# First RMSNorm of a hybrid decoder step: the raw rows turned by TensorE first, and the norm weight and row factor multiplied in afterwards

## The chip, the cores and the metric

The kernel runs on one core of one Trainium2 chip, in fp32. The metric is the device time of one execution in microseconds; three runs of the kernel before gave 590.5, 587.02 and 591.28 us. PE is TensorE, DVE is VectorE, ACT is ScalarE, POOL is GpSimd, SP is SyncE, which here mostly issues transfers.

## What is computed

One inference step of a two-layer decoder trunk over 320 tokens: a prompt of 256 and a sample group of 8 x 8. Layer 0 is sliding-window attention beside an S5 state space model, layer 1 is an RG-LRU beside dilated attention, and each is followed by a mixture of experts (16 experts, 2 per token). Every part begins with an RMSNorm of the residual rows. The change is in the first of them.

```python
def rmsnorm(x, g):
    xf = x.astype(F32)
    y = xf * lax.rsqrt(jnp.mean(xf * xf, axis=-1, keepdims=True) + RMS_EPS)
    return (y * g.astype(F32)).astype(x.dtype)

def even_mixer(h, kv_cache, s5_state, p, table):     # h = rmsnorm(x, norm_mix[0])
    proj = h @ p['w_in']                             # q, k, v for attention, u for S5
    ...
    ob, h_last = s5_mixer(u, h0, p)                  # lam_bar, b_bar and their powers: tables
```

## The kernel before, in words

The program is four blocks in a row: even_mixer_block (layer 0), moe_block, odd_mixer_block, moe_block. Within a block each engine has its own instruction stream, written out by hand, and waits on semaphores. An engine's stream is in order, so whatever stands behind a waiting instruction waits too.

The 320 tokens lie as rows in `resid`, in three tiles t = 0, 1, 2 of 128, 128 and 64 rows (`ROWS`), each row 1024 long. The projections need the normalised rows turned, with the 1024 features on the partitions: `xnT`, 8 chunks of 128 features by 320 tokens. The opening stage makes it so:

- SP issues, in this order, a small table input (L458), the three row tiles (L461), the norm weights and other columns (`small`, L462), the weights `w_u` (L152, from L463), the S5 B and C matrices (L464) and `w_qkv` (L152, from L465).
- POOL builds the identity matrix `ident` (L509 to L512).
- ACT and DVE make each row's sum of squares: DVE for tile 0 (L918), ACT for tiles 1 and 2 (`square`, L787). ACT takes the root of the mean (`root`, L793).
- DVE's `scale(t)` (L884 to L888) takes the reciprocal of the root and writes `rdiag[t]`, a diagonal matrix: the identity times the row factors.
- PE waits for tile 0 and for `ident`, runs three filler matmuls of 256 columns (`keep_clock_up`, L182; their results are not used), and then turns and scales in one step: for each tile eight matmuls of a 128-feature chunk of raw rows against `rdiag[t]` (L587), four to each of two PSUM banks, x0a, x0b, x1a, x1b, x2a, x2b.
- DVE's `gain(t)` (L890 to L899) multiplies each bank by the norm weight in one tensor_tensor of up to 512 columns (L896) and writes `xnT`. The weight is broadcast along the tokens, so one instruction serves four chunks.
- When x2b is emptied and `w_u` is there, PE starts the projections u0 to u3 (L577), then q0, eight banks of transposes of the S5 table `wt` (L602), q1, q2, the `tau` matmuls (L614), which need the S5 table `cp` that DVE finishes at L989, and then V (L625), q3, k and v.

An fp32 matmul is two MATMUL records in the profile and a transpose is one; so L587 has 24 matmuls and 48 records.

Between these steps DVE computes the small columns of the S5 discretisation (den, n1, cr, ci; L925 to L944; 16 columns each), and from L949 on it builds the large tables: `bbar`, `bbd`, `wt` (L970 to L975) and `cp` (L983 to L989). In the kernel before, den to cr (L925 to L935) stand between `scale(0)` and `scale(1)`, and three more (L942 to L944) behind the last gain. `Link` makes DVE wait for its own last instruction.

Names and lines that the steps touch: `rdiag` (L315), the semaphores (L402 to L405), POOL's identity (L509 to L512), PE's opening (L580 to L590), DVE's `scale` and `gain` (L884 to L899) and DVE's order of work (L924 to L944).

## Time and profile before

| | |
|---|---|
| three runs | 590.5, 587.02, 591.28 us; median 590.5 |
| span of the profiled execution | 585.1 us |
| PE busy | 560.8 us, 96% of the span |
| PEld (weight load) busy | 312.1 us, 53% |
| DVE busy | 250.1 us, 43% |
| ACT busy | 154.6 us, 26% |
| POOL busy | 77.0 us, 13% |
| moved by DMA | 208.96 MB, a mean of 357 GB/s |

The profiled execution's span runs from its first to its last instruction; the three runs are timed from outside and are 2 to 6 us longer. Start times in the rows below are us from the span's start. A row of the view in order of time gives the start, the time to the end of the last instruction of the group, engine, line, operation, output and input, shape and count; behind them, in brackets, the idle time before it and what ended it.

### The profile page before, as it was taken

Reading aid. Unit: us, or ns where it says so; the run is one execution under the profiler, and the core shown is the slowest. Engines: PE = TensorE matmul, PEld = TensorE weight load, DVE = VectorE, ACT = ScalarE, POOL = GpSimd, SP = SyncE. Lnnn points to the kernel's source line nnn. Section 1 sums busy time; section 2 is a strip of 40 time slices with the busy share of each in tenths; the row PEclk is TensorE's granted clock in tenths of the full one; section 3 lists DMA queues with packets and bytes.
Section 4 is the critical chain, followed back from the end, with each engine's and each line's share of the span. In section 5 each row is a group of like instructions: output and inputs, shape, how many; then the busy total and the mean of one; then the engine's idle time right before and its main releaser. Section 6 shows DMA issues by size and latency. Waiting matters only on the chain. (4 is left out here: it accounts for less than half of the span.)

```text
span 585.1 us, 8567 instructions
## 1 busy us (share of the span) xinstructions
PE 560.8 (96%) x3450; PEld 312.1 (53%) x3450; DVE 250.1 (43%) x595; ACT 154.6 (26%) x327; POOL 77.0 (13%) x116
## 2 busy tenths in 40 slices
PE   6999999999999999999999999999999899999992
PEld 5777876543633333337876556567644633333330
DVE  6999783224642112145633415350113751211147
ACT  6132195121301111134235105063013301011022
POOL 5940800000212110000000001000000021210000
PEclk9999999999999999999999999999999999999998
DMA  8995999997999999999999998999699989999982
GB/s 328 415 351 79 233 392 374 374 414 297 366 393 418 419 421 418 392 284 401 395 408 330 414 380 328 311 369 404 235 424 418 398 343 407 422 417 422 370 230 90
DMA packets 40074, 208.96 MB, mean 357 GB/s; under 512 B 12835, under 2 KB 14563, under 8 KB 24192
## 3 DMA queue, kind: packets, MB, share of 16 engines
q1 hardware_dynamic: 30560, 169.93, 75.1%
q0 software_dynamic: 7872, 34.53, 16.4%
q10 hardware_dynamic: 1600, 3.90, 1.7%
q8 instruction: 30, 0.49, 0.3%
q14 instruction: 12, 0.10, 0.0%
HBM read 198.77 MB, written 43.74 MB: 414 GB/s over the span
## 5 line engine op out<-in xcount | busy, mean ns | idle before, releaser
L1510 PE MATMUL bank<-arena 128*64 128x512 f32 x264 | 85.4, 598 | 0.2 <-DVE arena L1850 0.2
L1510 PE MATMUL bank<-ring,arena 128*64 128x512 f32 x232 | 74.4, 598 | 0.2 <-DVE arena L1850 0.2
L2326 PE MATMUL bank<-arena,ring 128*128 128x320 f32 x256 | 71.6, 434 | 0.0
L2326 PEld LDWEIGHTS bank<-arena,ring 128*128 128x128 f32 x256 | 48.0, 190 | 21.3 <-issue 1.6
L1431 PE MATMUL bank<-ring,arena 128*128 128x512 f32 x92 | 40.3, 594 | 1.0 <-PEq L455 0.6
L1510 PEld LDWEIGHTS bank<-arena 128*64 128x64 f32 x264 | 24.2, 136 | 31.4 <-issue 31.3
L1541 PE MATMUL bank<-arena 128*64 128x512 f32 x136 | 39.8, 594 | 0.7 <-ACT arena L1764 0.7
L577 PE MATMUL bank<-xnT,ring 128*128 128x320 f32 x144 | 39.5, 434 | 0.5 <-DVE xnT L896 0.5
L1984 DVE COPY arena<-bank 128x512 f32<-128x512 f32 x14 | 9.7, 692 | 68.3 <-PE bank L1541 68.3
L1541 PE MATMUL bank<-ring,arena 128*64 128x512 f32 x120 | 36.1, 593 | 0.7 <-ACT arena L1764 0.7
L1510 PEld LDWEIGHTS bank<-ring,arena 128*64 128x64 f32 x232 | 21.2, 136 | 24.7 <-issue 24.5
L577 PEld LDWEIGHTS bank<-xnT,ring 128*128 128x128 f32 x144 | 27.1, 190 | 11.6 <-DVE xnT L896 0.7
L1762 ACT ACTIVATE arena<-bank 128x256 f32<-128x256 f32 x16 | 6.1, 384 | 91.0 <-PE bank L1510 91.0
L1431 PEld LDWEIGHTS bank<-ring,arena 128*128 128x128 f32 x92 | 17.2, 190 | 22.7 <-issue 22.7
L1978 DVE TENSOR_TENSOR arena<-arena,bank 128x256 f32<-128x256 f32 x16 | 6.7, 421 | 51.9 <-ACT arena L1762 51.9
L1859 DVE TENSOR_TENSOR arena<-bank,small 128x512 f32<-128x512 f32 x28 | 18.1, 687 | 20.3 <-PE bank L1492 20.1
L1767 ACT COPY arena<-bank 128x512 f32<-128x512 f32 x16 | 9.4, 586 | 65.0 <-PE bank L1541 65.0
L1400 POOL DMA_INDIRECT y_rows<-arena x12 | 12.1, 1004 | 110.1 <-DVE arena L1984 110.1
L1541 PEld LDWEIGHTS bank<-arena 128*64 128x64 f32 x136 | 12.3, 136 | 20.7 <-issue 20.3
L2382 PE MATMUL bank<-ring,arena 128*128 128x512 f32 (+1 forms) x64 | 21.2, 489 | 0.0
L1746 ACT ACTIVATE arena<-resid 128x1024 f32<-128x1024 f32 (+1 forms) x6 | 6.3, 1058 | 54.8 <-DVE resid L1825 54.8
L1541 PEld LDWEIGHTS bank<-ring,arena 128*64 128x64 f32 x120 | 11.3, 136 | 16.3 <-issue 15.9
(450 smaller groups left out, 853.1 us busy)
## 6 DMA issues: line engine op xcount, KB each, us to landing
arena<-in_w_moe SPq DMA_DIRECT2D x50, 1024.0 KB, 16.8
ring<-in_w_moe SPq DMA_DIRECT2D x44, 1024.0 KB, 15.4
arena<-in_stream_b SPq DMA_DIRECT2D x4, 2560.0 KB, 14.6
out_o_d_old<-in_cache_d_g POOLq DMA_DIRECT2D x1, 8448.0 KB, 29.8
arena<-in_stream_a SPq DMA_DIRECT2D x4, 2048.0 KB, 10.4
out_o_d_old<-in_cache_d_g POOLq DMA_DIRECT2D x1, 7680.0 KB, 44.4
out_o_d_old<-in_cache_d_g SPq DMA_DIRECT2D x1, 4608.0 KB, 37.5
ring<-in_w_out_even SPq DMA_DIRECT2D x2, 2048.0 KB, 11.2
```

The lines of the kernel that those rows point to most:

```text
L577: last = nc.tensor.matmul(bank(name)[:, 0:TOK], lhs(k), c.xnT[:, k, :], start=(k == 0), stop=(k == KC - 1))
L1400: pool.indirect_dma_start(out=x["y_rows"], out_offset=bass.IndirectOffsetOnAxis(ap=scatter_idx[:, j:j + 1], axis=0), in_=yo_of(j), in_offs ...
L1431: last = nc.tensor.matmul(c.bank[2 * t + h][:, :], parts[q][:, t * P:(t + 1) * P], where[q][:, h * 512:(h + 1) * 512], start=(q == 0), sto ...
L1510: last = nc.tensor.matmul(c.bank[2 + j % 2][half, :], xgT[:, j % 2, q, half], w[i][q // 4][:, q % 4, :], start=(q == 0), stop=(q == KC - 1))
L1541: last = nc.tensor.matmul(c.bank[4 + h][half, :], hidT[:, j % 2, f, half], w[i][:, f, h * 512:(h + 1) * 512], start=(f == 0), stop=(f == 1))
L1746: nc.scalar.activation(xn[0:rows, t], c.resid[0:rows, t], ACT.Square, accum_out=c.stat[0:rows, t:t + 1]).then_inc(sq_ok, 1)
L1767: nc.scalar.copy(yo_of(j)[:, 0:512], c.bank[4][:, :]).then_inc(yo_a, 1)
L1859: v.tensor_tensor(xgT[:, j % 2, 4 * h:4 * h + 4, :], c.bank[h][:, :].rearrange("p (k r) -> p k r", k=4), c.gains[:, gain, 4 * h:4 * h + 4] ...
L1978: v.tensor_tensor(hid[:, j % 2], sg[:, j % 2], c.bank[2 + j % 2][:, FF:2 * FF], ALU.mult).then_inc(hid_ok, 1)
L1984: v.tensor_copy(yo_of(j)[:, 512:D], c.bank[5][:, :]).then_inc(yo_b, 1)
L2326: last = nc.tensor.matmul(bank(name)[:, 0:TOK], w[:, k, i * P:(i + 1) * P], xnT[:, k, :], start=(k == 0), stop=(k == KC - 1))
L2382: last = nc.tensor.matmul(bank(f"v{2 * t + n}")[:, 0:m], xnT[:, k, t * P:(t + 1) * P], wv[:, k, c0:c0 + m], start=(k == 0), stop=(k == KC ...
```

## The change

PE no longer waits for the row factors before it turns the rows. It turns each raw tile with plain transposes against `ident` as soon as that tile has landed (`turn_raw`). The row factors reach the other side by a second way: `row_factor(t)` is one matmul whose stationary operand is the column of factors broadcast to 128 columns and whose moving operand is `ident`; it leaves in bank 7, on every partition, the row of 128 (or 64) factors. DVE copies that row to SBUF (`factor`) and then multiplies each 128-feature chunk by the norm weight (a scalar per partition) and by the row of factors in one scalar_tensor_tensor: eight small instructions a tile in place of two large ones. `rdiag` is gone, `scale(t)` is the reciprocal alone. The three filler matmuls ahead of the turning go, and two stand behind each `row_factor` instead. On DVE the steps are interleaved, and most of the small S5 columns (the reciprocal of den to cr, and one more) move behind the last gain. POOL's wait inside the identity is written with another semaphore and is otherwise the same.

```diff
--- before.py
+++ after.py
@@ -312,7 +312,7 @@
     t["oS"] = f[:, 2560:2816]
     g = ar.take(4096)
     t["xn"] = g[:, 0:3 * D].rearrange("p (t d) -> p t d", t=3)
-    t["rdiag"] = g[:, 3 * D:3 * D + 3 * P].rearrange("p (t k) -> p t k", t=3)
+    t["factor"] = g[:, 3 * D:3 * D + TOK]
     t["win"] = g.rearrange("p (j r m) -> p j r m", r=2, m=P)
     t["S1"] = g[:, 0:2048].rearrange("p (h k) -> p h k", h=A_H)
     t["PT1"] = g[:, 2048:4096].rearrange("p (h b k) -> p h b k", h=A_H, b=2)
@@ -399,10 +399,11 @@
     ld_bc, ph_ok = c.sem("e_b_and_c"), c.sem("e_first_phases")
     ld_kc, ld_late, ld_bias = c.sem("e_kc"), c.sem("e_late"), c.sem("e_bias")
     full, a_empty, d_empty = c.sem("e_bank_full"), c.sem("e_act_emptied"), c.sem("e_dve_emptied")
-    ident0, ident_ok, bbd0, wuu0 = c.sem("e_ident0"), c.sem("e_ident"), c.sem("e_bbd0"), c.sem("e_wuu0")
+    ident_ok, bbd0, wuu0 = c.sem("e_ident"), c.sem("e_bbd0"), c.sem("e_wuu0")
     p_own, d_own, a_own = c.sem("e_pool_own"), c.sem("e_dve_own"), c.sem("e_act_own")
     dt_ok, arg_ok, trig_ok = c.sem("e_dt"), c.sem("e_arg"), c.sem("e_trig")
     sq_ok, rms_ok, xn_ok = c.sem("e_sq"), c.sem("e_rms"), c.sem("e_xn")
+    factor_pe = c.sem("e_pe_row_factor")
     lam_ok, pw_ok, rho_ok = c.sem("e_lambda"), c.sem("e_powers"), c.sem("e_rho")
     bbd_ok, wt_ok, cp_ok, h_ok = c.sem("e_bbd"), c.sem("e_wt"), c.sem("e_cp"), c.sem("e_h")
     u_out, u_in, wuu_in = c.sem("e_u_out"), c.sem("e_u_in"), c.sem("e_wuu_in")
@@ -418,7 +419,7 @@
     cp, wuu, wt, win, U, H, tau, y40 = (ev[n] for n in ("cp", "wuu", "wt", "win", "U", "H", "tau", "y40"))
     kcT, vc, bias, S0, SS, S1 = (ev[n] for n in ("kcT", "vc", "bias", "S0", "SS", "S1"))
     PT0, PTs, PTn, PT1, pw, ph, rho = (ev[n] for n in ("PT0", "PTs", "PTn", "PT1", "pw", "ph", "rho"))
-    rdiag = ev["rdiag"]
+    factor = ev["factor"]
     yT, ygT, xn, bbar, bbd, oS, vs = (ev[n] for n in ("yT", "ygT", "xn", "bbar", "bbd", "oS", "vs"))
     logdt, a_re, a_im = (ev["in"][:, PAIRS * q:PAIRS * (q + 1)] for q in range(3))
     braw, ct = (ev["in"][:, 3 * PAIRS + 512 * q:3 * PAIRS + 512 * (q + 1)].rearrange("p (r j c) -> p r j c", r=2, c=GC)
@@ -506,8 +507,7 @@
         @block.gpsimd
         def _(pool):
             g, link = nc.gpsimd, Link(pool, p_own)
-            g.memset(c.ident[:, :], 0.0).then_inc(ident0, 1)
-            pool.wait_ge(ident0, 1)
+            link(g.memset(c.ident[:, :], 0.0))
             g.affine_select(out=c.ident[:, :], in_=c.ident[:, :], compare_op=ALU.not_equal, fill=1.0,
                             base=0, pattern=[[-1, P]], channel_multiplier=1).then_inc(ident_ok, 1)
             g.memset(c.stat[:, 0:16], 1.0)
@@ -577,17 +577,32 @@
                     last = nc.tensor.matmul(bank(name)[:, 0:TOK], lhs(k), c.xnT[:, k, :], start=(k == 0), stop=(k == KC - 1))
                 last.then_inc(full, 1)
 
-            pe.wait_ge(ident_ok, 1)
-            pe.wait_ge(ld_x[0], 16)
-            c.keep_clock_up(c.bank[7], 3, 256)
-            for t, rows in enumerate(ROWS):
-                pe.wait_ge(xn_ok, t + 1)
+            def turn_raw(t):
+
+                rows = ROWS[t]
+                pe.wait_ge(ld_x[t], 16)
                 for h in range(2):
                     for k in range(4):
-                        last = nc.tensor.matmul(bank(f"x{t}{'ab'[h]}")[:, k * rows:(k + 1) * rows],
-                                                c.resid[0:rows, t, (4 * h + k) * P:(4 * h + k + 1) * P], rdiag[0:rows, t, 0:rows],
-                                                start=True, stop=True)
+                        last = nc.tensor.transpose(bank(f"x{t}{'ab'[h]}")[:, k * rows:(k + 1) * rows],
+                                                   c.resid[0:rows, t, (4 * h + k) * P:(4 * h + k + 1) * P], c.ident[0:rows, 0:rows])
                     last.then_inc(full, 1)
+
+            def row_factor(t):
+
+                rows = ROWS[t]
+                pe.wait_ge(xn_ok, t + 1)
+                nc.tensor.matmul(c.bank[7][:, t * P:t * P + rows], c.stat[0:rows, 6 + t:7 + t].broadcast_to([rows, P]),
+                                 c.ident[0:rows, 0:rows], start=True, stop=True).then_inc(factor_pe, 1)
+
+            pe.wait_ge(ident_ok, 1)
+            for t in range(3):
+                turn_raw(t)
+            row_factor(0)
+            c.keep_clock_up(c.bank[6], 2, 256)
+            row_factor(1)
+            c.keep_clock_up(c.bank[6], 2, 256)
+            row_factor(2)
+            c.keep_clock_up(c.bank[6], 2, 256)
             emptied(pe, "x2b")
             c.arrived(pe, IT_U)
             for i in range(4):
@@ -884,19 +899,20 @@
             def scale(t):
 
                 dve.wait_ge(rms_ok, t + 1)
-                link(v.reciprocal(c.stat[:, 6 + t:7 + t], c.stat[:, 3 + t:4 + t]))
-                v.tensor_scalar(rdiag[:, t], c.ident[:, :], c.stat[:, 6 + t:7 + t], None, ALU.mult).then_inc(xn_ok, 1)
-
-            def gain(t):
-
-                rows = ROWS[t]
-                for h in range(2):
-                    name = f"x{t}{'ab'[h]}"
-                    filled(dve, name)
-                    v.tensor_tensor(c.xnT[:, 4 * h:4 * h + 4, t * P:t * P + rows],
-                                    bank(name)[:, 0:4 * rows].rearrange("p (k r) -> p k r", k=4),
-                                    c.gains[:, 0, 4 * h:4 * h + 4].unsqueeze(2).broadcast_to([P, 4, rows]), ALU.mult)\
-                        .then_inc(d_empty, 1)
+                v.reciprocal(c.stat[:, 6 + t:7 + t], c.stat[:, 3 + t:4 + t]).then_inc(xn_ok, 1)
+
+            def gain(t, h):
+
+                rows, name = ROWS[t], f"x{t}{'ab'[h]}"
+                if h == 0:
+                    dve.wait_ge(factor_pe, t + 1)
+                    link(v.tensor_copy(factor[:, t * P:t * P + rows], c.bank[7][:, t * P:t * P + rows]))
+                filled(dve, name)
+                for k in range(4):
+                    last = v.scalar_tensor_tensor(c.xnT[:, 4 * h + k, t * P:t * P + rows], bank(name)[:, k * rows:(k + 1) * rows],
+                                                  c.gains[:, 0, 4 * h + k:4 * h + k + 1], factor[:, t * P:t * P + rows],
+                                                  ALU.mult, ALU.mult)
+                last.then_inc(d_empty, 1)
 
             dve.wait_ge(dt_ok, 1)
             v.tensor_tensor(x1, a_re, dt, ALU.mult).then_inc(arg_ok, 1)
@@ -921,24 +937,26 @@
             v.tensor_tensor(li, ex, sn, ALU.mult)
             v.tensor_tensor(lr, ex, cs, ALU.mult).then_inc(lam_ok, 1)
             dve.wait_ge(lam_ok, 1)
-            scale(0)
             v.tensor_tensor(t1s, a_re, a_re, ALU.mult)
             link(v.tensor_tensor(t2s, a_im, a_im, ALU.mult))
+            scale(0)
             link(v.tensor_tensor(den, t1s, t2s, ALU.add))
+            link(v.tensor_scalar(n1, lr, -1.0, None, ALU.add))
+            dve.wait_ge(ld_small, 16)
+            gain(0, 0)
+            scale(1)
+            gain(0, 1)
+            gain(1, 0)
+            scale(2)
+            gain(1, 1)
+            gain(2, 0)
+            gain(2, 1)
             link(v.reciprocal(den, den))
-
-            link(v.tensor_scalar(n1, lr, -1.0, None, ALU.add))
             v.tensor_tensor(t1s, n1, a_re, ALU.mult)
             link(v.tensor_tensor(t2s, li, a_im, ALU.mult))
             link(v.tensor_tensor(t1s, t1s, t2s, ALU.add))
             v.tensor_tensor(cr, t1s, den, ALU.mult)
             link(v.tensor_tensor(t2s, li, a_re, ALU.mult))
-            scale(1)
-            dve.wait_ge(ld_small, 16)
-            gain(0)
-            scale(2)
-            gain(1)
-            gain(2)
             link(v.tensor_tensor(t1s, n1, a_im, ALU.mult))
             link(v.tensor_tensor(t2s, t2s, t1s, ALU.subtract))
             link(v.tensor_tensor(ci, t2s, den, ALU.mult))
```

## Rows read from the trace of the kernel before

**Rows 1.** The page: span and busy time by engine
```profile
span 585.1 us, 8567 instructions
PE 560.8 (96%) x3450; PEld 312.1 (53%) x3450; DVE 250.1 (43%) x595; ACT 154.6 (26%) x327; POOL 77.0 (13%) x116
```
**Rows 2.** Busy by stretch: PE, PEld, DVE, ACT, POOL, granted clock, DMA share, GB/s
```profile
14.75:112.00 97.25, 97.17 (x904) 73.26 (x905) 73.11 (x116) 37.75 (x97) 33.70 (x32) 1.00 0.95 320
112.00:545.00 433.00, 424.83 (x2375) 220.66 (x2376) 148.75 (x419) 98.46 (x193) 33.55 (x42) 1.00 0.96 380
```
**Rows 3.** Waits of PE up to 120 us: us in total, times, longest
```profile
PE bank L577 <- DVE xnT L896: 0.5, 1, 0.5
```
**Rows 4.** In order of time, the opening stage
```profile
4.81 2.90 PE L182 MATMUL bank<-resid,ident 128*128 128x256 f32 x6 [4.81 <-DMA resid<-in_x_prompt]
7.02 0.16 DVE L887 RECIPROCAL stat<-stat 128x1 f32<-128x1 f32 x1 [0.75 <-ACT stat L793]
7.61 0.79 PE L587 MATMUL bank<-arena,resid 128*128 128x128 f32 x2
...
9.83 1.41 DVE L896 TENSOR_TENSOR xnT<-bank,small 128x512 f32<-128x512 f32 x2
14.27 0.42 DVE L896 TENSOR_TENSOR xnT<-bank,small 128x256 f32<-128x256 f32 x1 [0.47 <-PE bank L587]
14.75 21.80 PE L577 MATMUL bank<-xnT,ring 128*128 128x320 f32 x80 [0.52 <-DVE xnT L896]
15.27 0.42 DVE L949 TENSOR_TENSOR ring<-arena 128x256 f32<-128x256 f32 x1
```
**Rows 5.** In order of time, SP's issues of the row tiles and of w_u
```profile
1.20 0.89 SPq L461 DMA_DIRECT2D resid<-in_x_prompt  x2
2.13 0.57 SPq L461 DMA_DIRECT2D resid<-in_x_sample  x1
3.36 0.43 SPq L152 DMA_DIRECT2D ring<-in_w_u  x1
```
**Rows 6.** DMA issues of the same: count, KB each, median us from issue to landing
```profile
resid<-in_x_prompt SPq DMA_DIRECT2D x2, 512.0 KB, 4.1
resid<-in_x_sample SPq DMA_DIRECT2D x1, 256.0 KB, 5.4
ring<-in_w_u SPq DMA_DIRECT2D x1, 2048.0 KB, 9.1
```
**Rows 7.** In order of time, later on: the same filler, and transposes
```profile
152.48 1.03 PE L182 MATMUL bank<-resid,ident 128*128 128x256 f32 x4
36.39 3.66 PE L602 MATMUL bank<-ident,arena 128*128 128x128 f32 x32
148.08 0.70 PE L1450 MATMUL bank<-ident,resid 64*128 64x64 f32 x8 [0.42 <-DVE resid L1825]
```
**Rows 8.** Busy by stretch, columns as in Rows 2, while PE turns the tiles
```profile
10.00:11.00 1.00, 1.00 (x11) 1.00 (x10) 0.95 (x2) 0.93 (x3) 0.84 (x4) 1.00 0.92 393
```
**Rows 9.** In order of time: DVE, small steps with a scalar column, copies from PSUM
```profile
286.05 0.48 DVE L2683 SCALAR_TENSOR_TENSOR arena<-arena,small 128x256 f32<-128x256 f32 x1
286.45 0.28 DVE L2684 SCALAR_TENSOR_TENSOR arena<-arena,small 128x64 f32<-128x64 f32 x1
...
97.75 0.29 DVE L1079 COPY arena<-bank 128x128 f32<-128x128 f32 x1 [2.62 <-PE bank L749]
...
102.97 0.49 DVE L1082 COPY arena<-bank 128x128 f32<-128x128 f32 x2 [3.71 <-PE bank L764]
```
**Rows 10.** In order of time: the end of cp, the start of tau, DVE's next slack
```profile
45.05 2.56 DVE L989 SCALAR_TENSOR_TENSOR arena<-arena,ring 128x2304 f32<-128x2304 f32 x1
48.59 1.63 PE L614 MATMUL bank<-arena 128*32 128x128 f32 x52
69.89 1.29 DVE L1035 SCALAR_TENSOR_TENSOR arena<-bank,ring 128x512 f32<-128x512 f32 x2 [3.12 <-PE bank L645]
```
**Rows 11.** Instructions on bank, 4 to 20 us: ns min/median/max, first and last start
```profile
L587 PEld LDWEIGHTS bank<-arena,resid x48: 183/192/333, 7.6 to 13.9; 128*128 128x128 f32 x32, 64*128 64x128 f32 x16
```

## Prediction

> **What bounds the kernel now.** I read the page first: PE is busy for 560.8 of 585.1 us, and no other engine for half of that [rows 1]. Busy time alone doesn't say that PE sets the end, so I read the stretches next: from 14.75 to 112 us PE works for 97.17 of 97.25 us, and up to 545 us for 424.83 of 433 [rows 2]. From the first projection on PE has hardly a gap, so when that projection starts is worth its whole shift, unless something behind it comes late. PE's waits up to 120 us name, besides the first row tile, 0.5 us for DVE's last gain [rows 3]; the tile is there at 4.81 [rows 4]. The change lies in between, so the question is: when does the first projection (L577) start, 14.75 us before?
>
> The opening in order of time [rows 4] shows four things. Tile 0 is there at 4.8 us. The first row factor is there at 7.02 + 0.16 = 7.2, and PE turns with it from 7.61. DVE starts its gains at 9.83 and ends them at 14.27 + 0.42 = 14.69, 4.9 us later, with idle time in between because it waits for PE: PE sets the pace, DVE follows. w_u, issued at 3.36 [rows 5], takes 9.1 us [rows 6] and lands at 12.5; that is the earliest start a faster opening could reach, a gain of 2.2 us at most.
>
> **PE's clock.** The granted clock stands at 1.00 in every stretch [rows 2], but the fillers tell more. Six records of 256 columns take 2.90 us from 4.81 on [rows 4], and four of the same take 1.03 us at 152.48 [rows 7]. Taking away about 0.6 and 0.4 us for the last one's own length, one follows the other after 0.45 and 0.21 us: the slow level (1.2 GHz) at the start, the fast one (2.4 GHz) later. The rise lies between: from 10 to 11 us already 11 records of 128 columns run, less than 0.1 us each [rows 8], against 0.23 at the fillers' pace. PE had worked since 4.8 us. The projections are fast: 80 records of 320 columns in 21.80 us are 0.27 us each [rows 4].
>
> **The change, part by part, by its place in time.**
>
> *Turning the raw rows.* Removed are three fillers and the wait for the factor; added are 24 transposes. Tile 0 is there at 4.8; tile 1 is issued about 0.45 us after 1.20 and takes some 4.6 us (4.1 is the median of the two, and tile 0 took 3.6), so 6.3; tile 2 lands at 2.13 + 5.4 = 7.5 [rows 5, 6]. Fast, 32 transposes of 128 columns take 3.66 us, 0.11 each, and eight of 64 rows take 0.70, that is 0.07 each and 0.2 for the last one's length [rows 7]. PE is on the slow level here, and I take twice that: 16 x 0.227 = 3.6, then 8 x 0.13 = 1.1, and 4.8 + 4.7 = 9.5 us. The lower bound is the fast price: tile 2 is then the last to land, and 7.5 + 0.6 = 8.1.
>
> *The row factor stands behind all of them.* row_factor(0) is in PE's stream behind the 24 transposes, tile 2's wait included. Its input is ready at 7.3 and it runs at 9.5. A single fp32 matmul of 128 columns on the slow level is two records, 0.79 us from start to end [rows 4]. So DVE gets its first factor at 10.3 (lower bound 8.1 + 0.5 = 8.6), against 9.83 for its first bank before. The early turning buys nothing, since the factor doesn't come earlier than the matmul it replaces. DVE meanwhile has only den and n1 left, and idles from 8 to 10.3.
>
> *DVE's multiplications.* Removed are 6 large tensor_tensor (1.41 us for two of 512 columns [rows 4], so 4 x 0.7 + 2 x 0.42 = 3.6 us) and three rdiag of 0.3. Added are 24 scalar_tensor_tensor, 16 of 128 columns and 8 of 64, and three copies. The nearest rows, with the same kind of scalar column, are L2683 and L2684: 256 columns let the next start after 0.40 us [rows 9]. If a column costs 1/960 us, as from 256 to 64 columns (0.48 - 0.28 = 0.20 us for 192), then 0.133 us of it are fixed. A step of 128 costs 0.27 and one of 64 costs 0.20: 16 x 0.27 + 8 x 0.20 = 5.9 us. Copies: 0.29, 0.29 and 0.22 with 0.05 each for the link, 0.95. Reciprocals of tiles 1 and 2: 0.16 each, 0.32. Sum 7.2 us. The lower bound goes by copies of 128 columns without a scalar column, of which the second starts 0.20 after the first (two of 0.29 in 0.49 [rows 9]): 16 x 0.20 + 8 x 0.13 + 1.3 = 5.5. The upper bound, no overlap at all, is 0.35 and 0.28 a step: 9.1 us.
>
> *Are the later factors in time?* Tile 1's reciprocal stands behind gain(0, 0), so at 10.3 + 0.3 + 1.1 + 0.2 = 11.9. PE's two fillers run from 9.9 to 11.7, so it is free; the factor is out at 12.75, and DVE wants it at 12.95. For tile 2 the same sum gives 15.35 against 15.6. Both are hidden by gain(t, 1), with 0.2 us to spare; every tenth more on PE beyond that costs a tenth, twice.
>
> *The first projection.* 10.3 + 7.2 = 17.5, and 0.05 for the semaphore: 17.55 against 14.75, **2.8 us later**. w_u has long landed.
>
> *The moved S5 columns.* Nine small steps now stand behind the last gain where three stood. I take 0.21 each, estimated from the row factor's reciprocal of 0.16 [rows 4] and 0.05 for the link, 1.85 us in all. Table building starts at 17.5 + 1.85 = 19.3 instead of 15.27 [rows 4], 4.0 us later. From there DVE is busy without pause until cp ends at 45.05 + 2.56 = 47.6; PE wants it at 48.59 [rows 10]. PE is 2.8 late and has 1.0 to spare, 3.8 together, so the tau matmuls wait **0.2 us** more. Behind them DVE has 3.12 us of idle time at the first scores [rows 10], which takes up its remaining 1.0. The removed fillers cost PE nothing, since it waited then; the new ones lie in its waits for DVE. POOL's edit changes only a semaphore's name.
>
> **Sum.** 2.8 + 0.2 = 3.0 us, made against the profiled 585.1: 588.1. The median of the runs is 5.4 us above that execution, so 590.5 + 3.0 = **593.5 us**, 0.5% more. A measurement of this kernel can tell about 1% from no change, that is 5.9 us; the three runs alone lie 4.3 us apart.
>
> **Rivals.**
>
> *The clock has fallen, or never risen, when the projections start* (chance 0.13). Before, PE ran real matmuls without a pause from 4.8 us. After, 24 transposes come first, and then fillers with pauses; if the clock rises only for the latter, the projections may start slow. Before, PE was fast by 10 us [rows 8], some 5 us after its first matmul; if as much of the projections runs at half speed, 2.5 us are lost, so 3.0 + 2.5 = 5.5, and 596.0. Against it: from 9.5 us on the factor matmuls and fillers keep PE at work with short pauses only, for longer than it had worked before when it became fast. A rule speaks for this rival. The Trainium skill, page "TensorE: Matmul & The Clock Gate", Part 4, says that transposes don't count as work for the clock gate. The kernel before shows no stretch of transposes at the slow level, so its trace doesn't decide it; by the rule the clock's rise would only begin to be earned at 9.5.
>
> *Not slower: the opening is cheap* (chance 0.17). If transposes cost their fast price though the clock is slow, and DVE's steps come 0.20 apart, DVE starts at 8.6 and needs 5.5: 14.1, so 0.6 us earlier than before, and 589.9. It decides from the point where the first factor's time and DVE's steps add up to 14.7. With only one of the two true it is 590.5 + 1.1 or 1.3, and 591.7. Against it: while PE turned, the longest weight load took 333 ns and the median one 192 [rows 11], so I read the 333 as the slow level's, and the nearest steps with a scalar column have the larger fixed part. On this too a rule speaks otherwise: the Trainium skill, the same page, Part 2, gives a weight load of 128 columns about 107 ns, whatever the clock. By it tile 2's transposes would end at 8.4, the first factor would reach DVE at 9.2, and the sum would be 1.9 us instead of 3.0.
>
> *The shift is taken up later* (0.07): a wait on a transfer behind 14.75 us would make the change nothing, 590.5. Against it: PE's waits name none up to 120 us [rows 3].
>
> *DVE's tables become the bound* (0.03): if the moved columns or the slower gains make DVE more than 5 us late, tau waits for the difference, 1 to 2 us: 595. It starts at a lateness of DVE that is 1.0 us larger than PE's.
>
> **How the numbers follow.** The forecast keeps 0.60. Its own range is 592 to 595; with the cheap opening and the slow clock it is 589.9 to 596, and as medians of three runs move by some 2 us, I give 588.5 to 596.5. Faster by over 1% (under 584.6) is out of reach of every case, since w_u allows 2.2 us: 0.02. Slower by over 1% (over 596.4) needs the slow clock and high runs, or DVE's steps at their upper bound with it: 0.07. The rest, 0.91, is within 1%.
>
> **What would show it.** In the trace after: the last raw transpose starts near 9.4 and the first factor matmul follows; the first copy of the factor row is near 10.3, behind about 2 us of DVE idle time; steps of 128 columns start 0.27 apart; the first projection starts near 17.5 with 80 records in 21.8 us (more would be the slow clock); cp ends near 51.6, and tau starts just behind it. The forecast is wrong if the first factor comes by 8.6, if the steps are 0.20 apart, if the projections run at 0.45 us a record, or if the MoE stages begin at the old time although the projections don't.

## The result: 0.6% slower, and where it went

Over 13 runs each, the kernel before has a median of 589.93 us and the changed kernel of 592.45 us. Compared run for run the changed kernel takes 1.0062 times as long, 95% interval 1.0041 to 1.0082, which is 2.4 to 4.8 us. The forecast was 3.0 us more (1.0051) and 593.5 us. Ratios here and below leave out a run that lies more than 1.5% above the fastest of the same kernel: one of 660.39 us of the kernel before, and one of 594.03 us of the last version below.

The opening of the changed kernel, in order of time (start, length, engine, line, operation, shape, count; in brackets the idle time before and its end):

```profile
4.56 4.52 PE L586 MATMUL bank<-ident,resid 128*128 128x128 f32 x24 [4.56 <-DMA resid<-in_x_prompt]
...
7.07 0.16 DVE L902 RECIPROCAL stat<-stat 128x1 f32<-128x1 f32 x1 [0.45 <-ACT stat L808]
...
9.01 0.49 PE L594 MATMUL bank<-ident,stat 128*128 128x128 f32 x2
...
9.34 1.03 PE L182 MATMUL bank<-resid,ident 128*128 128x256 f32 x4
...
9.63 0.29 DVE L909 COPY arena<-bank 128x128 f32<-128x128 f32 x1 [2.05 <-PE bank L594]
...
9.96 1.13 DVE L912 SCALAR_TENSOR_TENSOR xnT<-bank,small,arena 128x128 f32<-128x128 f32 x4
...
14.80 1.62 DVE L912 SCALAR_TENSOR_TENSOR xnT<-bank,small,arena 128x64 f32<-128x64 f32 x8
...
16.48 5.92 PE L577 MATMUL bank<-xnT,ring 128*128 128x320 f32 x21 [1.32 <-DVE xnT L912]
...
18.22 0.42 DVE L967 TENSOR_TENSOR ring<-arena 128x256 f32<-128x256 f32 x1
```

These answer to [rows 4]. The factor is ready at 7.23 and its matmul runs at 9.01, behind all 24 transposes; DVE stands idle for 2.05 us until it can copy the factor row. From there to the end of its last small step at 16.42 it has no gap. The first projection starts at 16.48 instead of 14.75, 1.7 us later. The tables start at 18.22 instead of 15.27, 2.95 later.

The second stretch to look at lies between 18 and 57 us, where I had forecast almost nothing. In the kernel before its main steps are these:

```profile
17.81 0.85 DVE L962 COPY arena<-arena 64x512 f32<-64x512 f32 x2
...
32.84 3.51 POOL L549 MEMSET arena<- 128x4096 f32 x1
...
48.59 1.95 PE L614 MATMUL bank<-arena 128*32 128x128 f32 x64
```

In the changed kernel, again in order of time:

```profile
19.89 3.51 POOL L549 MEMSET arena<- 128x4096 f32 x1
20.32 0.42 DVE L972 TENSOR_TENSOR arena<-ring 128x256 f32<-128x256 f32 x1
20.78 3.34 DVE L980 COPY arena<-arena 64x512 f32<-64x512 f32 x2
...
41.61 8.78 PE L577 MATMUL bank<-xnT,ring 128*128 128x320 f32 x32
...
50.45 2.56 DVE L1007 SCALAR_TENSOR_TENSOR arena<-arena,ring 128x2304 f32<-128x2304 f32 x1
...
53.11 3.34 PE L629 MATMUL bank<-arena 128*32 128x128 f32 x64 [2.72 <-issue]
56.38 3.93 PE L640 MATMUL bank<-ring,arena 128*64 128x40 f32 x128
```

Two copies of 64x512 (they build `bbd`) take 3.34 us; in the kernel before two of them take 0.85. They begin while POOL's memset of 4096 columns is on (19.89 to 23.40) and end after it. In the kernel before that memset comes 13 us later, long behind the copies. So cp is ready at 50.45 + 2.56 = 53.01 instead of 47.61 [rows 10], 5.4 us later. PE is through with its projections at 50.39 and waits 2.72 us for it. Then the tau matmuls (L629) take 3.34 us, where those of the kernel before take 1.95: most of them at half speed. V (L640) starts at 56.38 instead of 50.47, so PE is now 5.9 us late: 1.7 from the opening, 2.7 from the wait, 1.4 from the slow tau, and 0.1 left over.

The stretches of PE show the clock's fall (length, busy time, granted clock, DMA share, GB/s):

```profile
50.40:53.10 2.70, 0.00 (x0) 0.91 0.00 0
53.10:56.40 3.30, 3.29 (x66) 0.56 0.02 5
56.40:60.20 3.80, 3.80 (x132) 1.00 0.03 6
```

The granted clock is 0.56 while the tau matmuls run, near the 1.2 GHz level, and 1.00 behind them. It fell within the 2.7 us in which PE stood idle (0.91 on the mean of that stretch).

The profiled pair is 6.8 us apart (585.1 and 591.9), more than the comparison of runs says. A second profile of each (below) gave 586.4 and 590.5, 4.1 us apart, as are their first MoE stages (114.42 and 118.54). The spread of single executions is part of what a single pair shows: over the profiles of all the kernels here, the stretch from the start of the first MoE stage to the end takes 471.3 to 474.6 us, and 478.5 in one.

### The profile page after: what moved, and what is told of

Read it like the earlier page. It is cut to its first block and busy times, and to the rows that moved or that the text cites. A ratio compares the mean times of both kernels' runs of the same rounds, so it can differ in the third digit from the quotient of the medians.

```text
span 591.9 us, 8563 instructions
## 1 busy us (share of the span) xinstructions
PE 561.6 (95%) x3438; PEld 311.8 (53%) x3438; DVE 254.6 (43%) x613; ACT 154.5 (26%) x327; POOL 64.0 (11%) x116
```

## The experiments

Each ratio is against the kernel before on the same chip. "Tables", "cp" and "tau" are the start of DVE's tables, the end of cp, and the start of the tau matmuls.

### POOL's memset later

```diff
+            pool.wait_ge(wt_ok, 2)
             g.memset(wuu, 0.0).then_inc(wuu0, 1)
```

> The changed kernel with one wait more: POOL clears wuu only when DVE has finished wt. Theory A (port collision): in the changed kernel POOL's 3.51 us memset from 19.89 holds up DVE's first bbd copy (2.90 us for what took about 0.43), cp ends 2.5 us later for it, tau waits 2.7 us and then runs slow (3.34 for 1.95 us). So here: first projection unchanged at 16.5, the two copies back to 0.85 us, cp ends near 50.6 instead of 53.0, tau waits 0.3 us at most and takes 1.95; the time falls by 3.5 to 4 us from the changed kernel's 592.5. Theory B (the moved columns alone make the tables late; the copy's length has another cause): cp and time don't move. Theory C (the profiled pair is 6.8 us apart by the spread of runs): no change in the median.

Measured: ratio 1.0026 (1.0002 to 1.0050), median 589.91. In order of time:

```profile
20.74 0.85 DVE L981 COPY arena<-arena 64x512 f32<-64x512 f32 x2
...
35.36 3.52 POOL L550 MEMSET arena<- 128x4096 f32 x1 [15.43 <-DVE arena L994]
...
47.93 2.56 DVE L1008 SCALAR_TENSOR_TENSOR arena<-arena,ring 128x2304 f32<-128x2304 f32 x1
...
50.59 1.95 PE L630 MATMUL bank<-arena 128*32 128x128 f32 x64
```

The opening is unchanged (first projection at 16.55), and everything behind it is as theory A wants: the copies back to 0.85 us, cp at 50.49, tau at 50.59 behind q2, at full speed. V starts at 52.47, 3.9 us earlier than in the changed kernel's first profile and 2.7 earlier than in its second (55.18, below), where tau ran at full speed. The time fell by 0.36% (1.0062 to 1.0026), some 2 us, less than the 3.5 to 4 that I expected: the slow tau, 1.4 of them, isn't in every run. The two intervals still overlap a little; that the collision is gone rests on the trace, and the size on the runs. The memset of 3.5 us lies here under DVE steps with two inputs (the cp tables), which keep their 2.55 us: it holds up only the copies.

### The copies as steps with two inputs

```diff
-                last = v.tensor_copy(bbd[...], bbar[rows])
+                last = v.tensor_tensor(bbd[...], bbar[rows], bbar[rows], ALU.max)
```

> The changed kernel with its two bbd copies (64x512) written as a tensor_tensor of bbar with itself (max), the same result, POOL's memset left where it is. In the changed kernel the tensor_tensor steps at 19.86 and 20.32 ran in their usual 0.42 us with the memset already on, and only the copy stood still. Theory A1 (the memset and a one-input DVE step exclude each other, a two-input step isn't held): both steps take about 0.6 us, cp ends near 50.7, tau waits 0.3 us at most, the time is that of the kernel with the late memset (589.9, 2 us less than the changed kernel). Theory A2 (any DVE step of that size is held while POOL clears): 2.9 us as before, cp at 53, no change.

Measured: ratio 1.0029 (1.0001 to 1.0058). The memset is where it was, and the two steps lie inside it:

```profile
19.30 3.51 POOL L549 MEMSET arena<- 128x4096 f32 x1
...
21.43 1.38 DVE L980 TENSOR_TENSOR arena<-arena 64x512 f32<-64x512 f32 x2
...
51.80 1.95 PE L629 MATMUL bank<-arena 128*32 128x128 f32 x64 [0.69 <-ACT arena L834]
```

1.38 us for two (0.69 each; two two-input steps of 512 columns take 1.41 in [rows 4]), nothing held, and cp at 51.70. That is 1 us later than expected: the first projection started at 17.21 here, since PE was at the slow level until past 12.5 us, and tau waited 0.69 us instead of 0.3 at most. Theory A1 holds: a one-input copy and the memset exclude each other, a two-input step and the memset don't. The ratio is that of the late memset; its interval is too wide to part it from the changed kernel by itself.

### The S5 columns back ahead of the gains

```diff
             link(v.tensor_scalar(n1, lr, -1.0, None, ALU.add))
+            link(v.reciprocal(den, den))
+            ... (t1s, t2s, cr, t2s)
             gain(0, 0)
             ...
             gain(2, 1)
-            link(v.reciprocal(den, den))
-            ... (t1s, t2s, cr, t2s)
```

> The changed kernel with the S5 columns (reciprocal of den to cr, and one more) back ahead of the gains, where DVE idles for 2 us. Theory A: first projection unchanged at 16.5, tables start at 17.0 instead of 18.2; the copies then start near 19.5, the second one still meets POOL's memset at 19.9, so cp ends between 51.7 and 52.5 and the time falls by about 0.7 to 1.5 us. Theory B: the whole lateness of the tables is the columns: cp ends 1.3 us earlier at 51.7, and the time falls by 1.3 us; nothing is left that a memset could explain.

Measured: ratio 1.0042 (1.0017 to 1.0067). In its profile:

```profile
16.78 8.63 PE L577 MATMUL bank<-xnT,ring 128*128 128x320 f32 x20 [1.33 <-DVE xnT L912]
...
19.94 0.95 DVE L980 COPY arena<-arena 64x512 f32<-64x512 f32 x2
...
20.55 3.79 POOL L549 MEMSET arena<- 128x4096 f32 x1
```

The tables started at 17.37 and the copies came just ahead of the memset, so the collision, which I had expected for the second one, didn't happen: this time POOL was held a little (3.79 for 3.51). cp ended at 49.78, 3.2 us earlier than in the changed kernel: 0.85 because the tables started earlier, 2.4 because the copies weren't held. Theory B, without a memset in it, had 51.7. But PE wasn't there to use it: 20 records of the projections took 8.63 us, 0.43 each, where the changed kernel's take 0.27. PE's clock fell in the pause of 1.33 us ahead of them (granted clock 0.94 from 15.4 to 16.1 us, 0.50 from 16.1 to 16.7), and the w transposes started at 41.40, 24.6 us behind the first projection instead of 21.6: the slow-clock rival, in one execution, at a price of 3.0 us. The runs show a gain of 0.2% over the changed kernel, less than the half-width of the interval, and can't decide between the theories; the trace speaks for A.

### Both repairs

The two edits together.

> The changed kernel with both repairs: S5 columns ahead of the gains, POOL's memset behind wt. What is left against the kernel before is the opening alone: first projection at 16.5 to 17.2 against 14.75, copies 0.85 us, cp near 49.4, no wait at tau. If the account is complete the time lies 1.7 us (0.3%) above the kernel before, as with the late memset alone (1.0026), since cp was then already just in time; if the columns had a cost of their own, it is lower than that by 0.3% and equals the kernel before.

Measured: ratio 1.0005 (0.9980 to 1.0030). First projection at 16.21, tables at 16.71, copies 0.86 us, cp at 49.00, tau at 50.05 without a wait, first MoE stage at 115.29 against 113.83 and 114.42 in the two profiles of the kernel before. What the opening itself costs is thus 0.9 to 1.5 us in the profile, and too little for the runs to tell. I expected 1.0026 if the columns cost nothing by themselves, and a ratio of 1 if they did. The interval holds both. By the profiles they cost little: the kernel with the late memset alone starts its MoE stage at 115.82, 0.5 us later, and 0.3 of that is there at its first projection.

### The column order alone, in the kernel before

```diff
             link(v.tensor_tensor(den, t1s, t2s, ALU.add))
-            link(v.reciprocal(den, den))
             link(v.tensor_scalar(n1, lr, -1.0, None, ALU.add))
-            ... (t1s, t2s, cr, t2s)
             scale(1)
             ...
             gain(2)
+            link(v.reciprocal(den, den))
+            ... (t1s, t2s, cr, t2s)
```

> The kernel before with only the order of DVE's S5 columns changed, as in the changed kernel. The first projection stays at 14.75 or comes 0.2 us earlier. Tables start near 16.5 instead of 15.3. Theory B: cp ends 1.2 us later, 48.8, tau waits 0.2 us, time up by 0.2 us. Theory A: POOL's memset, no longer held up by DVE's large steps, starts near 19.9, just as the bbd copies (19.1 to 19.9) end; if it catches the second one, cp ends near 51, tau waits 2.5 us and the time rises by 2.5 to 4 us; if it starts behind them, 0.2 us.

Measured: ratio 1.0006 (0.9981 to 1.0030). Tables at 16.42, copies at 19.02 to 19.88, free, cp at 48.81, tau at 48.91, 0.3 us later than in the kernel before: the 0.2 us of theory B, and 0.1 that this execution's first projection (14.85) was late. POOL's memset came at 22.61, because DVE's large steps, from 19.91 on, still reached the last small step of POOL's chain and held it for 2.24 us. The move of the columns is harmless alone; it takes the 1.7 us of the opening with it to open the gap in which POOL runs ahead.

### The first factor early

```diff
-            for t in range(3):
-                turn_raw(t)
-            row_factor(0)
+            turn_raw(0)
+            row_factor(0)
+            turn_raw(1)
+            turn_raw(2)
```

> The changed kernel with row_factor(0) right behind the transposes of tile 0 instead of behind all 24. My step said the first factor is late because it stands behind them: then the first factor row is copied near 8.2 instead of 9.6, and the first projection starts near 15.1 instead of 16.5. Tile 1's and 2's transposes are done by 10.4, in time for gain(1, 0). If DVE is held by something else (the later factors, or the steps), the start moves by under 0.5 us. On the time: 1.4 us less, or less than that where the tables (cp) set tau's start, since they also move by 1.4 us but may meet POOL's memset otherwise.

Measured: ratio 1.0041 (1.0020 to 1.0061).

```profile
4.55 1.94 PE L586 MATMUL bank<-ident,resid 128*128 128x128 f32 x8 [4.55 <-DMA resid<-in_x_prompt]
7.25 0.80 PE L594 MATMUL bank<-ident,stat 128*128 128x128 f32 x2 [0.76 <-DVE stat L903]
...
10.73 2.07 PE L182 MATMUL bank<-resid,ident 128*128 128x256 f32 x4
12.59 0.64 PE L594 MATMUL bank<-ident,stat 128*128 128x128 f32 x2
...
13.27 0.29 DVE L910 COPY arena<-bank 128x128 f32<-128x128 f32 x1 [2.54 <-PE bank L594]
...
17.66 7.61 PE L577 MATMUL bank<-xnT,ring 128*128 128x320 f32 x21 [1.32 <-DVE xnT L913]
```

Half of the expectation came true: the first factor row was copied at 8.18, 1.5 us earlier. The first projection didn't follow: it started at 17.66, not near 15.1. PE was still at the slow level at 10.7: the two fillers (four records) took 2.07 us instead of 1.03, row_factor(1) stood behind them, and DVE waited 2.54 us for its second factor. Whether the pause of 0.76 us ahead of the early factor kept the clock down isn't shown; two profiles without that pause were also slow at 9.4 us (below). The step is right that the factor is late for standing behind the transposes; in this execution undoing it only moved the wait to the next factor. The projections too ran in part at the slow level (granted clock 0.53 from 17.6 to 20 us), and yet the tau matmuls started at 53.18, as in the changed kernel (53.11): up to there cp sets the time, and a late PE is hidden. So this run doesn't price the order of the factors.

### Large steps in place of small ones

The norm weight is left out here, so a half tile needs one step, and the results are not those of the kernel; it serves as a price only:

```diff
-                for k in range(4):
-                    last = v.scalar_tensor_tensor(c.xnT[:, 4 * h + k, ...], bank(name)[...], c.gains[...], factor[...], ...)
+                last = v.tensor_tensor(c.xnT[:, 4 * h:4 * h + 4, ...], bank(name)[...], factor[...].unsqueeze(1).broadcast_to([P, 4, rows]), ALU.mult)
```

> The changed kernel with the late memset, and with the norm weight left out: each half tile is multiplied by the factor row alone, in one tensor_tensor of up to 512 columns instead of four scalar_tensor_tensor. It prices the step count by itself. If the 24 small steps are what the opening loses, DVE's gains take 4 x 0.62 + 2 x 0.35 = 3.2 us instead of 5.8, the first projection starts near 14.0 instead of 16.5, ahead of the 14.75 of the kernel before, and the time is 2.5 us under that of the kernel with the late memset (589.9) less what tau's wait for cp takes back. If the wait for the first factor is what is lost, the start moves by under 1 us.

Measured, with the late memset also in: ratio 0.9985 (0.9952 to 1.0018), against 1.0026 with the late memset alone: 2.4 us less, 2.5 expected, with intervals that overlap a little.

```profile
9.81 0.69 DVE L912 TENSOR_TENSOR xnT<-bank,arena 128x512 f32<-128x512 f32 x1
...
13.82 13.46 PE L578 MATMUL bank<-xnT,ring 128*128 128x320 f32 x49
```

The first projection started at 13.82, where the kernel with the late memset alone has 16.55. So the small steps cost 2.7 us of the opening, and the opening is 0.9 us ahead of the kernel before, in spite of the late first factor. A kernel that multiplies by the norm weight as well would need more than this; no run here prices it.

### No fillers

```diff
-            c.keep_clock_up(c.bank[6], 2, 256)      (three times)
```

> The changed kernel without its six filler matmuls. In its trace PE is fast already at the last transposes (8.4 us), so the transposes alone brought the clock up. If it then stays up over pauses of 1.5 us and more, the first projection starts at 16.5 and runs at 0.27 us a record without fillers too, and the time doesn't change. If PE's work between 9 and 16.5 us holds the clock, three small matmuls aren't enough: the first projection's records take 0.54 us until the clock rises again, 20 in 8.6 us as in the profile of the kernel with the columns moved back, and the time rises by 2 to 3 us.

Measured: ratio 1.0055 (1.0029 to 1.0080), that of the changed kernel. Its profile:

```profile
9.36 0.79 PE L594 MATMUL bank<-ident,stat 128*128 128x128 f32 x2
11.87 0.80 PE L594 MATMUL bank<-ident,stat 128*128 128x128 f32 x2 [1.71 <-DVE stat L899]
...
17.13 10.30 PE L577 MATMUL bank<-xnT,ring 128*128 128x320 f32 x31 [2.13 <-DVE xnT L909]
...
21.34 2.10 DVE L977 COPY arena<-arena 64x512 f32<-64x512 f32 x2
...
40.46 3.66 PE L614 MATMUL bank<-ident,arena 128*128 128x128 f32 x32
...
52.66 1.96 PE L626 MATMUL bank<-arena 128*32 128x128 f32 x64
```

The factor matmuls ran at the slow level (0.79 us), and part of the projections too: 23.3 us up to the w transposes instead of 21.6, 1.7 more. In the changed kernel's two profiles, with fillers, the projections ran fast. Yet the runs don't show it, and the profile says why. The copies meet the memset here as well (2.10 us for two), cp ends at 52.33, and PE, late by its slow records, comes to the tau matmuls at 52.66 with hardly a wait; V starts at 54.54, earlier than in either profile of the changed kernel (56.38 and 55.18). As long as cp is that late, what PE loses ahead of tau, up to 2.7 us, doesn't reach the end. The clock ahead of the projections also varies with fillers in, as the kernel with the columns moved back showed. What the fillers are worth stays open.

### Second profiles of both kernels

> The kernel before, unchanged, for a second profile. Its first profile (span 585.1) is some 2.7 us under its median, and single profiles of kernels that agree to 0.4 us at the first MoE stage (113.8 against 114.2) lie 7.6 us apart at the end. If the spread is made late, in the transfers of y rows and the routing behind the first MoE stage, this profile agrees with the first to 0.3 us up to 114 us, and the difference opens between 160 and 290 us. If it is made in the opening, the first projection or tau start elsewhere than at 14.75 and 48.6.

> The changed kernel, unchanged, for a second profile. The first projection depends on when PE's clock rises: 16.5 to 17.2. POOL's memset should again meet the bbd copy (first copy near 21, memset from 19 to 23), so cp ends between 52 and 53 and tau waits 1 to 3 us more than in the kernel before. The slow tau (3.34 us) comes only if the clock falls in that wait, which I give one chance in two.

The kernel before started its projections at 15.34 this time, not at 14.75, since PE's turning took 7.19 us instead of 6.62. The clock rose later: from 9.6 to 10.6 us PE ran 7 records, against 12 in the first profile. That is a miss of the expectation, which put the whole spread behind 160 us: 0.6 us of it are made in the opening. The rest is made later, as expected: a matmul of the first MoE stage (L1492) is at 164.21 in the first profile and at 166.30 in the second, and 1.3 us of the 2.1 are left at the end. The changed kernel repeats what its first profile showed, but for the slow tau:

```profile
16.04 11.30 PE L577 MATMUL bank<-xnT,ring 128*128 128x320 f32 x41 [1.32 <-DVE xnT L912]
...
20.09 3.51 POOL L549 MEMSET arena<- 128x4096 f32 x1
20.17 4.14 DVE L980 COPY arena<-arena 64x512 f32<-64x512 f32 x2
...
53.30 1.96 PE L629 MATMUL bank<-arena 128*32 128x128 f32 x64 [2.90 <-issue]
```

The copies took 4.14 us and tau waited 2.90 us in this execution too, at a granted clock of 1.00: the collision is in both executions, the fall of the clock is not. Two bounds of the expectation were missed by a little: the first projection came at 16.04, below 16.5, and cp ended at 53.20, above 53.

### A version that beats both

On the kernel before; the rows are scaled ahead of the turning, in one DVE step a tile, and turned by plain transposes. DVE's order changes as well, which these lines don't show: the S5 columns from the reciprocal of den on stand behind the last gain, and scale(2) between the two halves of gain(0):

```diff
-                v.tensor_scalar(rdiag[:, t], c.ident[:, :], c.stat[:, 6 + t:7 + t], None, ALU.mult).then_inc(xn_ok, 1)
+                v.tensor_scalar(xn[0:ROWS[t], t], c.resid[0:ROWS[t], t], c.stat[0:ROWS[t], 6 + t:7 + t], None, ALU.mult)...
-                        last = nc.tensor.matmul(bank(...)[...], c.resid[0:rows, t, ...], rdiag[0:rows, t, 0:rows], ...)
+                        last = nc.tensor.transpose(bank(...)[...], xn[0:rows, t, ...], c.ident[0:rows, 0:rows])
+            c.keep_clock_up(c.bank[7], 2, 256)
```

> A version meant to beat both, on the kernel before: DVE multiplies the raw rows of a tile by their factor in one tensor_scalar of 1024 columns (as the other norms of this kernel do), PE turns them with plain transposes (24 records in place of 48), and the six large gains stay. The S5 columns stand behind the gains, two fillers behind the last transpose. If PE's fp32 matmuls against rdiag set the pace before, and DVE's step count after, this opening needs three steps of about 0.6 us more and three of 0.33 less on DVE, and DVE ends its gains near 13.1 instead of 14.7: first projection near 13.2, tables at 15.0, cp near 47.5, tau right behind q2: 1.5 us less than the kernel before. Rival: the 1024-column steps are held up by POOL, which runs small steps all that time, or cp sets tau's start at 48.6 as before; then 0 to 0.5 us less.

Measured: ratio 0.9964 (0.9940 to 0.9987), median 587.56: 0.8 to 3.5 us faster than the kernel before.

```profile
7.25 0.81 DVE L888 TENSOR_SCALAR arena<-resid,stat 128x1024 f32<-128x1024 f32 x1
...
13.51 13.73 PE L577 MATMUL bank<-xnT,ring 128*128 128x320 f32 x50 [0.69 <-DVE xnT L896]
...
47.73 1.96 PE L614 MATMUL bank<-arena 128*32 128x128 f32 x64 [0.31 <-issue]
```

The tensor_scalar steps took 0.75 to 0.83 us, not 0.6, and the first projection is at 13.51, 1.2 us earlier than before. Now cp (47.63) sets tau's start, with a wait of 0.31. V starts 0.85 us earlier than in the kernel before (49.62 against 50.47), at the low end of what the runs give. The profiled execution as a whole was longer than that of the kernel before (586.2 against 585.1), by the spread behind the first MoE stage; the gain at the end rests on the runs.

## Why the prediction was right, and where its sum was not

**What bounds the kernel: right.** The shift of PE passed through: 4.1 us between the second profiles at the first MoE stage and 4.1 at the end, 5.9 and 6.8 between the first. With a spread of 3 us behind the first MoE stage the equal numbers of the second pair are partly chance; that the shift isn't taken up is shown by the runs, 2.4 to 4.8 us.

**The first factor behind all transposes: right, its size too large.** The transposes ended at 9.1 instead of 9.5, and the factor matmul took 0.49 instead of 0.79, so the first copy was at 9.63 instead of 10.3. The term that was mis-sized is the clock: I took the slow level for the whole opening. Weight loads of tile 2, of the same shape, show both levels. In the changed kernel (the last row is tile 2):

```profile
4.53 1.56 PEld L586 LDWEIGHTS bank<-ident,resid 128*128 128x128 f32 x8 [4.53 <-issue]
...
6.56 1.57 PEld L586 LDWEIGHTS bank<-ident,resid 128*128 128x128 f32 x8 [0.46 <-DMA resid<-in_x_prompt]
...
8.37 0.58 PEld L586 LDWEIGHTS bank<-ident,resid 64*128 64x128 f32 x8 [0.24 <-issue]
```

Tile 2 in the kernel without fillers:

```profile
8.32 0.93 PEld L586 LDWEIGHTS bank<-ident,resid 64*128 64x128 f32 x8 [0.33 <-issue]
```

Eight loads take 0.58 us in the one and 0.93 in the other, and in the changed kernel the fillers behind them (1.03 us for four records) are at the fast level, as in [rows 7]. Where the level stayed slow the forecast of 10.3 was met: the first copy came at 10.29 without fillers and at 10.37 with the two-input copies. Two smaller errors nearly cancel. Eight transposes of 128 columns on the slow level take 1.56 us, one every 0.19, so 0.23 was 0.04 too much; against it the sum had no room for the 0.46 and 0.24 us that PE stood idle ahead of tiles 1 and 2. The Trainium skill's 107 ns for a weight load of 128 columns ("TensorE: Matmul & The Clock Gate", Part 2), which it gives for either level, was too little by more: the trace has one every 190 ns at the slow level.

**DVE's steps: right.** Sixteen of 128 columns came 0.26 apart (0.27 forecast), eight of 64 at 0.19 (0.20). From the first copy to the end of the last step 6.8 us (7.2 forecast); the kernel with large steps shows by subtraction that their number costs 2.7 us. The later factors were in time, as forecast.

**The first projection: 16.48, forecast 17.55.** 1.7 us later than before instead of 2.8: 0.7 of the difference came with the first factor, 0.4 with DVE's steps. In the two profiles with the slow opening it was 17.13 and 17.21.

**The moved columns: right, and harmless alone.** The nine small steps took 1.87 us (1.85 forecast). Tables 2.95 us late instead of 4.0, for the 1.1 us just named.

**The wait at tau: the step that failed.** Forecast 0.2 us, measured 2.7 and 2.9, and in one profile 1.4 more for the slow clock. "From there DVE is busy without pause until cp ends" was taken over from the kernel before, as if DVE's table work were a block of fixed length that only starts later. It isn't: POOL works beside it. In the kernel before POOL's chain of small steps was slowed by DVE, two rows of POOL in order of time:

```profile
18.82 2.24 POOL L519 TENSOR_TENSOR arena<-arena 128x16 f32<-128x16 f32 x1
21.02 2.26 POOL L520 TENSOR_TENSOR arena<-arena 128x16 f32<-128x16 f32 x1
```

Sixteen columns took 2.24 us there, as long as DVE's step of 2048 columns beside them, and 0.2 us where DVE had no large step. Six such steps put POOL's memset off to 32.84 us, under DVE's cp steps, which it doesn't hold. In the changed kernel DVE's large steps come so late that POOL's chain is through at 19.6; the memset starts at 19.89 and meets the two one-input copies. The late memset and the two-input copies each undo it by another way, and both bring the ratio from 1.0062 to 1.003. With the late memset PE is through at 50.47, cp is ready at 50.49 and tau starts at 50.59: without the collision the forecast of 0.2 us holds. I wrote of POOL only that its edit was a semaphore's name; its place in time was never asked.

The Trainium skill, page "SBUF — State Buffer", section "Who interferes with whom", would have warned me: it says that DVE and POOL take turns on a shared pair of ports, for a whole instruction, when DVE runs a copy in its two-port mode, or a step with two SBUF inputs while POOL reads SBUF; a POOL instruction that only writes doesn't disturb the latter. That the copies ran in that mode no view names; it fits that one of 512 columns takes 0.43 us where a two-input step takes 0.69. The traces agree on the rest: the copies held until a memset's end (3.34 and 4.14 us instead of 0.85), the two-input steps not held by it (0.42 and 2.55 us unchanged), POOL's reading steps held by two-input steps (2.24 us).

**The rivals.** The slow clock at the projections did occur, in the profile of the kernel with the columns moved back (3.0 us; 2.5 forecast) and in part without fillers and with the early factor (1.7 each), but not in either profile of the changed kernel. The rule that spoke for it fell: see below. The cheap opening didn't happen; the early transposes bought nothing. "DVE's tables become the bound" was given 0.03 and a price of 1 to 2 us, from a lateness of DVE 1.0 us larger than PE's; it is what happened, by a cause that I had not named. So the sum of 3.0 came near the measured 3.7 (0.62%) in part by luck, with two errors of opposite sign: 1.1 us too much in the opening, and 2.5 too little at tau. By the runs the two parts are 1.5 us (what is left with the late memset) and 2.1 (what the late memset takes away).

## What to carry to other kernels

Moving work on one engine by a microsecond also moves it against its neighbour on the shared port: before costing a block as "the same, only later", look at what POOL runs beside it, and which of the two started first. Breaking a large DVE step into four for the sake of a per-partition scalar costs some 0.13 us a step (estimated: 0.26 us from start to start, less 128 columns at the pace of [rows 9]); here that was 2.7 us, more than the 2.2 that the early start could ever have given. Early work gains nothing while the value that everything waits for (the row factor) stands behind it in an in-order queue. And an experiment on one engine can be blind: while cp was late, what PE lost ahead of tau didn't reach the end. Scaling the rows first and turning them afterwards was the faster order.

## What the hardware showed that I had not expected

**Transposes raise PE's clock.** In the changed kernel PE does nothing but transposes from 4.56 to 9.0 us, and by tile 2's it is at the fast level: 0.58 us for eight weight loads, which take 0.93 in the kernel without fillers, and, behind them, 1.03 us for the four filler records, which take 1.91 with the two-input copies. In five other profiles with this opening the first fillers take 1.03 us as well; in two (two-input copies, no fillers) PE is still at the slow level at 9.4 us, so the moment is not the same in every execution. The Trainium skill, page "TensorE: Matmul & The Clock Gate", Part 4, says that transposes don't count as work there; the measurement decides, and in this fp32 kernel they do.

**The pause that costs the clock.** After 2.7 us of idle time ahead of tau the granted clock was 0.56 in one profile, and after 2.9 us 1.00 in another. Ahead of the projections a pause of 1.33 us ended at 0.50 with the columns moved back, and one of 1.32 at 1.00 in the changed kernel. Not every fall can be read from the length of the pause ahead of it. The moment of the rise varies as well: in the kernel before PE's turning took 6.62 us in one execution and 7.19 in the next.

**The granted clock of the profile misses the slow level of the opening.** It stands at 1.00 there while the fillers run at half speed, and in the kernel without fillers it stands at 1.00 up to 20 us, where six records of the projections take 2.87 us (at 0.27 each they would take 1.6); in the fall at tau it shows it (0.56). The spacing of records of one shape is the surer sign.
